# mLSTM denominators: the decayed scores are added over the key tiles on VectorE, and the ones matrix is multiplied with the one block of sums

## The chip, the cores and the metric

The kernel runs on one NeuronCore of a Trainium2 chip. The metric is device time in microseconds (us) of one execution, lower is better. TensorE (PE) multiplies matrices, VectorE (DVE) and ScalarE (ACT) do elementwise work, GpSimd (POOL) does some elementwise work and issues a few transfers, SyncE (SP) issues the weight loads. The engines run side by side and meet at semaphores.

## The reference

A trunk of two layers over 528 tokens (16 meta tokens and 512 of the sequence) with 1024 features. Layer 0 is an mLSTM mixer with 8 heads and a squared-ReLU MLP; layer 1 is differential attention and another MLP. What bears on the change is the denominator of the mLSTM:

```python
d_mat = jnp.exp(log_d - m_t[..., None])                        # decay, causal
s = jnp.einsum('bhctd,bhcsd->bhcts', qc, kc) * d_mat           # decayed scores
num = inter * (q @ C_prev) + einsum('bhcts,bhcse->bhcte', s, vc)
den = inter * (q @ n_prev) + jnp.sum(s, axis=-1)               # sum over the keys
hh = num / jnp.maximum(jnp.abs(den), jnp.exp(-m_t))[..., None]
```

The kernel computes it without chunks and carries: for each head a full causal table of decayed scores, 528 queries by 528 keys, whose sum over all keys is `den`.

## The kernel before

Everything is held transposed: features or keys on the 128 partitions, tokens along the row. Operands of TensorE that need full fp32 are split into a high and a low fp32r part, so that a product of a weight with an activation takes three passes (high·high, high·low, low·high). One weight unit is 128 output features: 8 blocks of 128 input features, 3 passes, 2 token halves of 264, thus 48 matmuls. `wh` and `wl` hold the two parts of a unit; ACT makes `wh` from the loaded `raw` (the copy in `split_unit`) and DVE subtracts to get `wl` (`split`, L814). The result of a unit is taken out of PSUM by DVE with `scaled` (L833). From head 1 on every unit of the mLSTM projections uses the same two PSUM banks 0 and 1, so that a unit can start only when the one before it has been taken out.

Each head has three units: unit 0 gives its q and k (to `qkf`), unit 1 its v (to `vf0`), unit 2 its output gate (to `of`). The eight heads are software-pipelined: the step of head hd does the scores and the outputs of head hd, and the three units of head hd+1. The order on each engine is written out by hand in the four functions `step0`. I call TensorE's stages in the step of head hd:

- **scores**: keys by queries (L1262), 14 matmuls, to `ps` banks 2 to 5
- **unit 0** of head hd+1: 48 matmuls
- **values**: the weighted sum of v, 21 matmuls (L1245 with `vh` and `vl`), after `p_ready`, to banks 6 and 7 (`B_ND`)
- **unit 1** of head hd+1, after DVE has taken unit 0 out
- **denominators**: the ones matrix times the decayed scores (L1245 with `ones_r`), 14 matmuls, to the same two banks as the values. It waits for `num_rd`: ACT has read the values.
- **unit 2, first half**: 24 matmuls, after DVE has taken unit 1 out (`evac`)
- **mean squares** over the features (L1294), 4 matmuls, after ACT has squared the denominators (`den_sq`) and DVE has made `sql`
- **unit 2, second half**, then the **transposes** of v (L1315), then the scores of head hd+1

The decayed scores of a head stand in `dmat`, 1360 columns: seven pieces, one for each key tile and query range of the causal table (`PIECES`, their first columns in `DCOL`). Five of them hold scores of queries from 256 on (of 272, 272, 272, 144 and 16 columns), the other two those of queries 0 to 255 and 128 to 255. DVE first fills `dmat` for the next head with exponents (`exponents`, 7 instructions, L899), ACT takes their exponential (L533), POOL masks the diagonal blocks (L437), and DVE multiplies by the scores (L912, L916). ACT then copies `dmat` to `phi` (three pieces) and DVE makes `plo` = `dmat` - `phi` (L923), after which `p_ready` is signalled.

In the step of a head DVE's order is: L912/L916, `plo`, take out unit 0 (`qkf`), finish the log-sigmoid of the gate (L931, waits for `lsig`), `exponents`, three subtractions for the stacked q and k (L942 to L944, wait for ACT's three copies), two `wl` splits, take out unit 1 (`vf0`), a third split, `sql`, and then the work on the denominators. ACT's order is: the three `phi` copies, three functions for the log-sigmoid (L555, L557, L559, the `lsig` chain), three copies of q and k, the exponential of `dmat`, two `wh` splits, the reading of the values (four instructions, L589 and L590, which signal `num_rd`), `sqh`, an exponential (L539), a third split, and the squares of the denominators (L602, L603).

Loops are register loops over pairs of heads (`heads_loop`): heads 1 to 6 run in the loop, heads -1, 0 and 7 outside. In the step of head 7 there is no next head, and the units are the first ones of the output projection.

Of the kernel before, what the change touches and what calls it, by code (L numbers as in the profile page):

```python
# [30 lines left out]
ALU = mybir.AluOpType  # L31
ACT = mybir.ActivationFunctionType
AX = mybir.AxisListType
F32 = mybir.dt.float32
# [71 lines left out]
def wait(eng, sem, value):  # L106

    if not isinstance(value, int) or value > 0:
        eng.wait_ge(sem, value)
# [20 lines left out]
def program(nc, a, out):  # L130
    with ExitStack() as ctx:
# [4 lines left out]
        def place(name, shape, dt, where, end):  # L136
            size = 2 if dt == BF16 else 4
            for n in shape[1:]:
                size *= n
            size = (size + 31) // 32 * 32  # L140
            assert where[0] + size <= end, (name, where[0] + size - end)
            t = nc.alloc_sbuf_tensor_at(name, shape, dt, offset=where[0])
            where[0] += size
            return t

        def new(name, shape, dt=F32):
# [43 lines left out]
        sqh, sql = (place(n, [P, T], F32R, w0, limit) for n in ("sqh", "sql"))  # L190
        dmat = place("dmat", [P, DW], F32, w0, limit)
        phi, plo = (place(n, [P, DW], F32R, w0, limit) for n in ("phi", "plo"))
        ks, qhs, qls, vh, vl, of, mbc, nmbc = (
            [place(f"{name}{par}", shape, dt, w0, limit) for par in range(2)]
            for name, shape, dt in (("ks", [P, T], F32R), ("qhs", [P, T], F32R), ("qls", [P, T], F32R),
# [37 lines left out]
        def sems(names):  # L233
            return [sem(n) for n in names.split()]
# [21 lines left out]
            "stack_hi stack_lo v_t dpre dexp dready emn_done")  # L256
        s_done, p_ready, pv_done, den_done, num_rd, den_sq, x_rd, ssq_done, t_rd = sems(
            "s_done p_ready pv_done den_done num_rd den_sq x_rd ssq_done t_rd")
        lsig, w_done, hln_done, e_done, rs_rd, z_mul, zh_rd, z_ready = sems(
            "lsig w_done hln_done e_done rs_rd z_mul zh_rd z_ready")  # L260

# [197 lines left out]
        def _(act):  # L459
# [81 lines left out]
            def step0(hd, par, pair):  # L541
                n1, nxt = hd + 1, exists(hd + 1)
                first = isinstance(hd, int) and hd < 0
                if exists(hd):

                    wait(act, den_done, hd)
                    for n, (c0, c1) in enumerate(P_CUTS):
                        act.wait_ge(p_done, hd * len(P_CUTS) + (n + 1))
                        rows = 16 if c0 == D_FULL else P
                        copy(phi[0:rows, c0:c1], dmat[0:rows, c0:c1]).then_inc(ph_done, 1)  # L550
                if exists(hd):

                    act.wait_ge(evac, hd * 3 + 3)
                    wait(act, w_done, hd)
                    nc.scalar.activation(tbuf[:, :], of[par][:, :], ACT.Abs).then_inc(lsig, 1)  # L555
                    act.wait_ge(lsig, hd * 3 + 1)
                    nc.scalar.activation(tbuf[:, :], tbuf[:, :], ACT.Exp, scale=-1.0).then_inc(lsig, 1)  # L557
                    act.wait_ge(lsig, hd * 3 + 2)
                    nc.scalar.activation(tbuf[:, :], tbuf[:, :], ACT.Ln, bias=1.0).then_inc(lsig, 1)  # L559
                if nxt:  # L560

                    act.wait_ge(evac, n1 * 3 + 1)
                    wait(act, s_done, hd)
                    copy(ks[1 - par][0:64, :], qkf[64:128, :])
                    copy(qhs[1 - par][0:64, :], qkf[0:64, :])
                    copy(qhs[1 - par][64:128, :], qkf[0:64, :]).then_inc(stack_hi, 1)
                    if first:

                        act.wait_ge(u_t, 1)
                        copy(ucol[:, 0:4, :], ps[:, B_SUM, 0:32].rearrange("p (s g) -> p s g", s=4))  # L570
                        copy(ucol[0:16, 4, :], ps[0:16, B_SUM, 32:40])
                        copy(gains[:, 32:56], ps[:, B_SUM, 64:88]).then_inc(ucol_rd, 1)
                    else:
                        decays(n1, par)
                        split_unit(n1 * 3 + 2, 2, 0, n1)
                    split_unit(n1 * 3 + 3, 0, 0, n1 + 1)
                elif exists(hd):

                    act.wait_ge(unit_done, U_OUT0)
                    split(U_OUT0 + 2, 2, 0)  # L580
                    split(U_OUT0 + 3, 3, 0)
                if exists(hd):

                    act.wait_ge(pv_done, hd + 1)

                    wait(act, z_ready, hd)
                    wait(act, ssq_done, hd)
                    for b, t0, t1 in ((B_ND, 0, QSPLIT), (B_ND + 1, QSPLIT, T)):
                        copy(nf[:, t0:t1], ps[:, b, 0:t1 - t0], gains[:, ds(hd + 32, 1)])  # L589
                        last = nc.scalar.activation(abuf[:, t0:t1], ps[:, b, 0:t1 - t0], ACT.Square)  # L590
                    last.then_inc(num_rd, 1)

                    act.wait_ge(num_rd, hd + 1)
                    copy(sqh[:, :], abuf[:, :]).then_inc(sq_hi, 1)
                if nxt:
                    if not first:
                        row(par, pair)
                        split_unit(n1 * 3 + 4, 1, 0, n1 + 1)
                if exists(hd):

                    act.wait_ge(den_done, hd + 1)
                    nc.scalar.activation(acc[:, 0:QSPLIT], ps[:, B_ND, 0:QSPLIT], ACT.Square)  # L602
                    nc.scalar.activation(acc[:, QSPLIT:T], ps[:, B_ND + 1, 0:T - QSPLIT], ACT.Square).then_inc(den_sq, 1)  # L603

                    act.wait_ge(t_rd, hd + 1)
                    nc.scalar.activation(acc[:, :], acc[:, :], ACT.Ln).then_inc(hln_done, 1)
                    act.wait_ge(e_done, hd + 1)
                    nc.scalar.activation(acc[:, :], acc[:, :], ACT.Exp).then_inc(rs_rd, 1)
                if nxt:

                    act.wait_ge(v_t, n1 + 1)
                    wait(act, pv_done, hd)
                    copy(vh[1 - par][:, 0:4, :], ps[:, B_ND, :].rearrange("p (s e) -> p s e", e=P))
                    copy(vh[1 - par][0:16, 4, :], ps[0:16, B_ND + 1, 0:P]).then_inc(vh_done, 1)
                if first:
                    split_unit(4, 1, 0, 1)
                    decays(0, 1)
                    row(1, -1)
                if exists(hd):
                    act.wait_ge(z_mul, hd + 1)  # L620
                    copy(ah[:, ds(hd, 1), :].rearrange("p o t -> p (o t)"), nf[:, :]).then_inc(zh_rd, 1)
# [184 lines left out]
        def _(dve):  # L806
# [86 lines left out]
            def exponents(n1, par, pair):  # L893
# [6 lines left out]
                                           ucol[0:rows, j, ds(n1, 1)], 0.0, ALU.subtract, ALU.max)  # L900
                last.then_inc(dpre, 1)

            def step0(hd, par, pair):
                n1, nxt = hd + 1, exists(hd + 1)
                first = isinstance(hd, int) and hd < 0
                if exists(hd):

                    dve.wait_ge(s_done, hd + 1)
                    dve.wait_ge(dready, hd + 1)
                    dm = dmat  # L910
                    for n, (b, w, c0) in enumerate(P_BANKS):
                        ins = V.scalar_tensor_tensor(dm[:, c0:c0 + w], ps[:, b, 0:w], SCORE_SCALE, dm[:, c0:c0 + w],  # L912
                                                     ALU.mult, ALU.mult)
                        if n in (1, 3):
                            ins.then_inc(p_done, 1)
                    V.scalar_tensor_tensor(dm[0:16, D_FULL:DW], ps[0:16, B_S0 + 3, 272:288], SCORE_SCALE,  # L916
                                           dm[0:16, D_FULL:DW], ALU.mult, ALU.mult).then_inc(p_done, 1)

                    wait(dve, den_done, hd)
                    for n, (c0, c1) in enumerate(P_CUTS):  # L920
                        rows = 16 if c0 == D_FULL else P
                        dve.wait_ge(ph_done, hd * len(P_CUTS) + (n + 1))
                        last = V.tensor_tensor(plo[0:rows, c0:c1], dm[0:rows, c0:c1],  # L923
                                               phi[0:rows, c0:c1].bitcast(F32), ALU.subtract)
                    last.then_inc(p_ready, 1)
                    if nxt:

                        scaled(n1 * 3, 0, ALL, qkf[:, :])

                    dve.wait_ge(lsig, hd * 3 + 3)  # L930
                    V.scalar_tensor_tensor(of[par][:, :], of[par][:, :], 0.0, tbuf[:, :], ALU.min, ALU.subtract).then_inc(w_done, 1)  # L931
# [250 lines left out]
        def _(pe):  # L1182
# [67 lines left out]
            def step0(hd, par, pair):  # L1250
# [28 lines left out]
                if exists(hd):  # L1279

                    pe.wait_ge(num_rd, hd + 1)
                    one = lambda rows, j: ones_r[0:rows, :]
                    weighted(par, ((one, False), (one, True)), den_done)
                if nxt:
                    part0(n1, 2, 0, 4)
                else:
# [322 lines left out]
```

## Time before, and the profile before

| what | value |
|---|---|
| median of 3 runs | 1306.67 us (1305.73 to 1308.74) |
| span of the profiled execution | 1303.2 us |
| median of the runs less that span | 3.5 us |
| TensorE busy | 1278.0 us, 98% of the span |
| VectorE busy | 682.4 us, 52% |
| ScalarE busy | 544.9 us, 42% |
| GpSimd busy | 65.8 us, 5% |
| mean granted TensorE clock | 0.995 |
| the eight mLSTM heads | about 46 to 246 us |

No time of its own is given for the profiled execution beside its span; the span goes from the first to the last instruction, and the runs' times lie 3.5 us above it. Busy shares are means over the whole kernel. In the timeline an instruction's row gives its start, its length and, in square brackets, how long the engine sat idle before it and what ended that. Matmuls and elementwise instructions overlap their successor's start, so the cost of one in a queue is the distance from its start to the next one's start, which is less than its length.

### The profile page before, as it was taken

The numbers are of one execution on the slowest core, as the hardware profiler recorded it, in microseconds if no ns is written. First come the engines' busy times: TensorE is split into PE (matmuls) and PEld (weight loads), VectorE is DVE, ScalarE is ACT, GpSimd is POOL, SyncE is SP. The second block draws the span as 40 slices with busy tenths as digits, with TensorE's granted clock in tenths as the row PEclk, the third lists the DMA queues.
The fourth block names the chain that finished last, engine by engine and source line by source line (L and its number), as shares of the span: only waits on it lengthen the run. The fifth ranks groups of instructions, "written<-read, shape, count | busy, mean of one in ns | idle before, by whom it ended". The sixth has DMA issues, their size and how long they took to land.

```text
span 1303.2 us, 20870 instructions
## 1 busy us (share of the span) xinstructions
PE 1278.0 (98%) x8381; PEld 1153.7 (89%) x8381; DVE 682.4 (52%) x992; ACT 544.9 (42%) x895; POOL 65.8 (5%) x90
## 2 busy tenths in 40 slices
PE   7999999999999999999999999998999999999997
PEld 6899999999999999999988888876888888888886
DVE  5877777654334334234556677663643343443443
ACT  4656655543214123123445566664532241231332
POOL 3321221000000000000000000000000000000000
PEclk9899999999999999999999999999999999999999
DMA  6352242222232322222321211210332323232311
GB/s 161 84 122 72 65 111 75 71 75 89 96 97 98 98 65 97 97 91 70 97 81 50 65 49 48 64 64 33 97 97 98 97 98 97 97 97 97 97 65 64
DMA packets 141574, 110.28 MB, mean 85 GB/s; under 512 B 22104, under 2 KB 139920, under 8 KB 141520
## 3 DMA queue, kind: packets, MB, share of 16 engines
q1 hardware_dynamic: 140000, 104.93, 26.2%
q0 software_dynamic: 1392, 4.49, 1.5%
q8 instruction: 39, 0.64, 0.2%
q14 instruction: 15, 0.12, 0.0%
q10 hardware_dynamic: 128, 0.09, 0.0%
HBM read 107.38 MB, written 2.13 MB: 84 GB/s over the span
## 4 chain that ended last, share of the span: by engine, by line
issue 53%; PE 42%; DVE 2%; ACT 1%; DMA 0%; POOL 0%; SPq 0%; DVEq 0%; POOLq 0%; ACTq 0%
PE ps L1196 38%; PE ps L1245 2%; PE ps L1262 1%; DMA raw<-in_mlstm_w_in_dram 0%; DVE wl L814 0%; POOL dmat L437 0%; DVE yl L856 0%; PE ps L1315 0%; PE ps L1348 0%; PE ps L1294 0%; ACT wh L461 0%; DVE fin L1178 0%; DVE h L841 0%; PE ps L1212 0%; POOL sql L454 0%
## 5 line engine op out<-in xcount | busy, mean ns | idle before, releaser
L1196 PE MATMUL ps<-yh,wh 128*128 128x264 f32 (+1 forms) x1472 | 368.1, 314 | 0.5 <-DVE wl L814 0.4
L1196 PE MATMUL ps<-yl,wh 128*128 128x264 f32 (+1 forms) x1472 | 361.7, 309 | 0.0
L1196 PE MATMUL ps<-yh,wl 128*128 128x264 f32 (+1 forms) x1472 | 360.8, 309 | 0.0
L461 ACT ACTIVATE wh<-raw 128x1024 fp32r<-128x1024 f32 x192 | 200.1, 1049 | 188.4 <-PE ps L1196 187.9
L814 DVE TENSOR_TENSOR wl<-raw,wh 128x1024 fp32r<-128x1024 f32 x192 | 240.1, 1254 | 55.3 <-ACT wh L461 53.3
L1196 PE MATMUL ps<-ah,wh 128*128 128x264 f32 (+1 forms) x960 | 257.6, 322 | 1.3 <-DVE al L1167 0.8
L1196 PE MATMUL ps<-al,wh 128*128 128x264 f32 (+1 forms) x960 | 257.0, 322 | 0.0
L1196 PE MATMUL ps<-ah,wl 128*128 128x264 f32 (+1 forms) x960 | 256.3, 321 | 0.0
L1196 PEld LDWEIGHTS ps<-yh,wh 128*128 128x128 f32 x1472 | 239.7, 189 | 17.2 <-issue 1.7
L1196 PEld LDWEIGHTS ps<-yh,wl 128*128 128x128 f32 x1472 | 239.2, 189 | 13.7
L1196 PEld LDWEIGHTS ps<-yl,wh 128*128 128x128 f32 x1472 | 239.5, 189 | 13.0 <-issue 0.2
L1196 PEld LDWEIGHTS ps<-ah,wh 128*128 128x128 f32 x960 | 159.7, 188 | 16.5 <-DVE al L1167 1.2
L1196 PEld LDWEIGHTS ps<-ah,wl 128*128 128x128 f32 x960 | 159.3, 188 | 13.7
L1196 PEld LDWEIGHTS ps<-al,wh 128*128 128x128 f32 x960 | 159.4, 188 | 13.3
L1003 DVE TENSOR_TENSOR h<-ps,h 128x528 f32<-128x528 f32 (+1 forms) x80 | 55.9, 699 | 213.8 <-PE ps L1196 213.8
L646 ACT ACTIVATE abuf<-tbuf 128x528 f32<-128x528 f32 (+1 forms) x64 | 40.9, 639 | 267.3 <-DVEq L1028 267.3
L1025 DVE SCALAR_TENSOR_TENSOR tbuf<-ps,rb 128x528 f32<-128x528 f32 (+1 forms) x64 | 44.8, 700 | 113.0 <-PE ps L1196 107.3
L1030 DVE TENSOR_TENSOR al<-abuf,ah 128x528 fp32r<-128x528 f32 (+1 forms) x64 | 44.9, 701 | 82.6 <-ACT ah L647 82.6
L461 ACT ACTIVATE yh<-h,gains 128x528 fp32r<-128x528 f32 (+1 forms) x32 | 23.4, 731 | 59.6 <-DVEq L1008 52.7
L697 ACT ACTIVATE e<-ps,stat 128x272 f32<-128x272 f32 (+3 forms) x48 | 26.6, 557 | 47.1 <-DVE stat L1084 44.9
L454 POOL TENSOR_TENSOR sql<-abuf,sqh 128x512 fp32r<-128x512 f32 x8 | 10.3, 1290 | 646.6 <-ACT sqh L461 646.6
L647 ACT ACTIVATE ah<-tbuf 128x528 fp32r<-128x528 f32 (+1 forms) x64 | 39.8, 622 | 0.0
(196 smaller groups left out, 1072.6 us busy)
## 6 DMA issues: line engine op xcount, KB each, us to landing
raw<-in_mlp_w_up_dram SPq DMA_DIRECT2D x32, 1024.0 KB, 5.2
raw<-in_mlp_w_down_dram SPq DMA_DIRECT2D x32, 1024.0 KB, 4.9
raw<-in_diff_w_in_dram SPq DMA_DIRECT2D x24, 512.0 KB, 3.8
raw<-in_mlstm_w_in_dram SPq DMA_DIRECT2D x16, 512.0 KB, 3.9
raw<-in_mlstm_w_in_dram SPq DMA_DIRECT2D x16, 256.0 KB, 4.1
raw<-in_mlstm_w_out_dram SPq DMA_DIRECT2D x3, 1024.0 KB, 4.9
raw<-in_diff_w_out_dram SPq DMA_DIRECT2D x3, 1024.0 KB, 5.0
mbc<-gate_rows POOLq DMA_DIRECT2D x8, 264.0 KB, 4.5
```

What stands on the lines that cost most here:

```text
L454: nc.gpsimd.tensor_tensor(sql1[:, :], abuf[:, NMETA:T], sqh1[:, :].bitcast(F32), ALU.subtract).then_inc(sq_lo1, 1)
L461: return nc.scalar.activation(o, i, ACT.Copy, scale=scale)
L646: nc.scalar.activation(abuf[:, t0:T], tbuf[:, t0:T], ACT.Square).then_inc(sqa_done, 1)
L647: nc.scalar.activation(ah[:, k, t0:T], tbuf[:, t0:T], ACT.Square).then_inc(ah_done, 1)
L697: nc.scalar.activation(dst, src, ACT.Exp, bias=stat[:, i % 2, c:c + 1], accum_out=stat[:, i % 2, 2 + c:3 + c]).then_inc(exp_done[c], 1)
L814: V.tensor_tensor(wl[:, k, :, :], raw[:, k // 2, :, P * (k % 2):P * (k % 2) + P], wh[:, k, :, :].bitcast(F32), ALU.subtract).then_inc(spli ...
L1003: ins = V.tensor_tensor(tokens(h[:, b, :], spans), src or banks(k, spans), tokens(h[:, b, :], spans), ALU.add)
L1025: V.scalar_tensor_tensor(tokens(tbuf[:, :], spans), banks(k, spans), 0.0, tokens(rb[:, :], spans), ALU.max, ALU.mult).then_inc(evac, 1)
L1030: V.tensor_tensor(al[:, k, t0:T], abuf[:, t0:T], ah[:, k, t0:T].bitcast(F32), ALU.subtract).then_inc(a_ready, 1)
L1196: last = mm(ps[:, bank + s, 0:w_], w[:, slot, kb, :], m[:, kb, t0:t0 + w_], start=(kb == 0 and n == 0), stop=(kb == CB - 1 and n == 2))
L1245: last = mm(ps[:, b, c:c + t1 - t0], what(rows, j), p, start=(b not in seen), stop=(n in (1, len(PIECES) - 1) and i == len(passes) - 1))
L1262: last = mm(ps[0:rows, b, c:c + t1 - t0], ks[par][:, s0:s0 + rows], q[:, t0:t1], start=(m == 0), stop=(m == 1))
```

## The change

The multiplication by the ones matrix sums over the 128 partitions, that is over the keys of one tile; PSUM accumulates over the tiles. After the change DVE first adds the pieces of `dmat` that belong to the same queries and different key tiles into one block `dsum` of 528 columns (`column_sums`: five additions and a copy, and three of the additions wait for the one before them). ACT copies `dsum` to the high part `dsh`, DVE subtracts to get the low part `dsl`, and TensorE multiplies the ones matrix by `dsh` and `dsl` in 4 matmuls where it had 14.

`column_sums` stands on DVE between `plo` and the taking out of unit 0; the subtraction for `dsl` stands right after unit 0. On ACT the copy to `dsh` stands between the `phi` copies and the log-sigmoid. TensorE waits for `dsl_done` beside `num_rd`. As `phi` and `plo` are now last read by the values, they wait for `pv_done` and no longer for `den_done`; `dsum` waits for `den_done`.

```diff
+        dsum_at = w0[0]
+        dsum = place("dsum", [P, T], F32, w0, limit)
+        dsl = place("dsl", [P, T], F32R, [dsum_at], limit)
+        dsh = place("dsh", [P, T], F32R, w0, limit)
...
 # ScalarE, step0
-                    wait(act, den_done, hd)
+                    wait(act, pv_done, hd)
                     for n, (c0, c1) in enumerate(P_CUTS):
                         act.wait_ge(p_done, hd * len(P_CUTS) + (n + 1))
                         rows = 16 if c0 == D_FULL else P
                         copy(phi[0:rows, c0:c1], dmat[0:rows, c0:c1]).then_inc(ph_done, 1)
+                if exists(hd):
+
+                    act.wait_ge(dsum_done, hd + 1)
+                    copy(dsh[:, :], dsum[:, :]).then_inc(dsh_done, 1)
                 if exists(hd):
 
                     act.wait_ge(evac, hd * 3 + 3)
...
 # VectorE
+            def column_sums(hd):
+                d = dsum
+                at = lambda n: dmat[:, DCOL[n]:DCOL[n + 1]]
+
+                wait(dve, den_done, hd)
+                V.tensor_tensor(d[:, 128:256], dmat[:, 128:256], at(1), ALU.add)
+                V.tensor_copy(d[:, 0:128], dmat[:, 0:128])
+                V.tensor_tensor(d[:, 256:528], at(2), at(4), ALU.add).then_inc(dsum_first, 1)
+                dve.wait_ge(dsum_first, hd * 3 + 1)
+                V.tensor_tensor(d[:, 256:528], d[:, 256:528], at(5), ALU.add).then_inc(dsum_first, 1)
+                dve.wait_ge(dsum_first, hd * 3 + 2)
+                V.tensor_tensor(d[:, 384:528], d[:, 384:528], at(3), ALU.add).then_inc(dsum_first, 1)
+                dve.wait_ge(dsum_first, hd * 3 + 3)
+                V.tensor_tensor(d[0:16, 512:528], d[0:16, 512:528], dmat[0:16, D_FULL:DW], ALU.add).then_inc(dsum_done, 1)
...
-                    wait(dve, den_done, hd)
+                    wait(dve, pv_done, hd)
                     for n, (c0, c1) in enumerate(P_CUTS):
...
                     last.then_inc(p_ready, 1)
+                    column_sums(hd)
                     if nxt:
 
                         scaled(n1 * 3, 0, ALL, qkf[:, :])
+
+                    dve.wait_ge(dsh_done, hd + 1)
+                    V.tensor_tensor(dsl[:, :], dsum[:, :], dsh[:, :].bitcast(F32), ALU.subtract).then_inc(dsl_done, 1)
 
                     dve.wait_ge(lsig, hd * 3 + 3)
...
 # TensorE, step0
                     pe.wait_ge(num_rd, hd + 1)
-                    one = lambda rows, j: ones_r[0:rows, :]
-                    weighted(par, ((one, False), (one, True)), den_done)
+                    pe.wait_ge(dsl_done, hd + 1)
+                    for b, t0, t1 in ((B_ND, 0, QSPLIT), (B_ND + 1, QSPLIT, T)):
+                        for m, d in enumerate((dsh, dsl)):
+                            last = mm(ps[:, b, 0:t1 - t0], ones_r[:, :], d[:, t0:t1], start=(m == 0), stop=(m == 1))
+                    last.then_inc(den_done, 1)
```

## Rows read from the trace of the kernel before

**Rows 1.** Timeline of TensorE, heads 2 and 3: start, length, line, operation, count.

```profile
116.73 0.51 PE L1196 MATMUL ps<-yh,wh 128*128 128x264 f32 x2
...
133.87 0.51 PE L1196 MATMUL ps<-yh,wh 128*128 128x264 f32 x2
...
139.83 0.28 PE L1245 MATMUL ps<-phi,ones_r 128*128 128x256 f32 x1
...
141.67 0.51 PE L1196 MATMUL ps<-yh,wh 128*128 128x264 f32 x2
...
144.70 0.28 PE L1294 MATMUL ps<-sqh,head_mean 128*128 128x256 f32 x1
...
145.20 0.41 PE L1196 MATMUL ps<-yh,wh 128*128 128x264 f32 x2
```

**Rows 2.** Timeline of VectorE, heads 3 and 4.

```profile
128.28 1.70 DVE L923 TENSOR_TENSOR plo<-dmat,phi 128x800 fp32r<-128x800 f32 x3 [0.18 <-ACT phi L461]
131.40 0.71 DVE L833 TENSOR_TENSOR qkf<-ps,rb 128x528 f32<-128x528 f32 x1 [1.43 <-PE ps L1196]
132.03 0.70 DVE L931 SCALAR_TENSOR_TENSOR of<-of,tbuf 128x528 f32<-128x528 f32 x1
132.64 1.69 DVE L899 TENSOR_SCALAR dmat<-mbc,ucol 128x256 f32<-128x256 f32 x7
...
136.78 2.95 DVE L814 TENSOR_TENSOR wl<-raw,wh 128x1024 fp32r<-128x1024 f32 x2 [0.28 <-ACT wh L461]
...
142.30 0.70 DVE L960 TENSOR_TENSOR sql<-abuf,sqh 128x528 fp32r<-128x528 f32 x1
...
153.34 1.70 DVE L923 TENSOR_TENSOR plo<-dmat,phi 128x800 fp32r<-128x800 f32 x3 [0.31 <-ACT phi L461]
```

**Rows 3.** Timeline of ScalarE, head 3.

```profile
134.37 1.33 ACT L533 ACTIVATE dmat<-dmat 128x1344 f32<-128x1344 f32 x1 [0.27 <-DVE dmat L899]
...
135.70 1.99 ACT L461 ACTIVATE wh<-raw 128x1024 fp32r<-128x1024 f32 x2
137.60 0.45 ACT L461 ACTIVATE nf<-ps,gains 128x256 f32<-128x256 f32 x1
...
138.59 0.37 ACT L590 ACTIVATE abuf<-ps 128x272 f32<-128x272 f32 x1
```

**Rows 4.** Timelines of ScalarE and VectorE, head 7: the log-sigmoid.

```profile
228.64 0.63 ACT L555 ACTIVATE tbuf<-of 128x528 f32<-128x528 f32 x1
...
230.65 0.71 DVE L931 SCALAR_TENSOR_TENSOR of<-of,tbuf 128x528 f32<-128x528 f32 x1 [0.77 <-ACT tbuf L559]
```

**Rows 5.** Groups by form, 60 to 260 us: count, busy us, mean ns.

```profile
L461 ACT ACTIVATE sqh<-abuf 128x528 fp32r<-128x528 f32 x8 | 5.2, 646 | 0.3
...
L912 DVE SCALAR_TENSOR_TENSOR dmat<-ps,dmat 128x272 f32<-128x272 f32 x14 | 5.4, 431 | 0.0
```

**Rows 6.** Timeline of VectorE: instructions that wait for their predecessor on VectorE.

```profile
40.10 0.70 DVE L885 TENSOR_TENSOR gnm<-gb,gm 8x528 f32<-8x528 f32 x1
40.83 0.42 DVE L887 TENSOR_SCALAR gnm<-gnm 8x528 f32<-8x528 f32 x1
...
254.64 1.23 DVE L814 TENSOR_TENSOR wl<-raw,wh 128x1024 fp32r<-128x1024 f32 x1 [0.15 <-DVE h L1003]
```

**Rows 7.** Timelines of VectorE and TensorE, head 0.

```profile
54.40 1.70 DVE L923 TENSOR_TENSOR plo<-dmat,phi 128x800 fp32r<-128x800 f32 x3 [0.18 <-ACT phi L461]
...
66.87 0.52 PE L1196 MATMUL ps<-yh,wh 128*128 128x264 f32 x2
```

**Rows 8.** Timelines of GpSimd in head 3 and of VectorE in head 7.

```profile
135.88 4.35 POOL L437 TENSOR_TENSOR dmat<-dmat,causal 128x128 f32<-128x128 f32 x5 [14.95 <-ACT dmat L534]
...
231.60 2.36 DVE L814 TENSOR_TENSOR wl<-raw,wh 128x1024 fp32r<-128x1024 f32 x2 [0.24 <-ACT wh L461]
```

**Rows 9.** Windows: busy us of PE, PEld, DVE, ACT, POOL; PEclk; DMA share; GB/s.

```profile
42.00:44.00 2.00, 0.77 (x9) 0.52 (x7) 1.21 (x3) 1.95 (x5) 1.03 (x3) 1.00 0.10 17
...
48.00:50.00 2.00, 2.00 (x12) 1.92 (x11) 2.00 (x7) 1.08 (x1) 0.00 (x0) 0.50 0.75 166
```

More of the change, by code:

```diff
@@ L258, in program @@
             "s_done p_ready pv_done den_done num_rd den_sq x_rd ssq_done t_rd")
+        dsum_first, dsum_done, dsh_done, dsl_done = sems("dsum_first dsum_done dsh_done dsl_done")
         lsig, w_done, hln_done, e_done, rs_rd, z_mul, zh_rd, z_ready = sems(
```

## The prediction

> **What bounds the kernel now.** I read the page first, for the busy shares, then the timeline of TensorE in the mLSTM heads, then those of VectorE and ScalarE beside it. TensorE is busy for 98% of the span (the table above). In the heads it goes without a gap: the first half of unit 2 starts at 116.73 in head 2 and at 141.67 in head 3, a period of 24.94 us, in which one stage begins where the last one ends [rows 1]. So time taken from TensorE there counts in full, as long as DVE and ACT keep up. How near they are to being late is the question, and it is read stage by stage in head 3.
>
> After `plo` ends (128.28 + 1.70 = 129.98) DVE idles 1.43 us until unit 0 is finished, at 131.40 [rows 2]. ACT reads the values until 138.59 + 0.37 = 138.96 [rows 3], and the denominators, which wait for that in the same banks, start at 139.83 [rows 1]: 0.87 us to spare. `sql` is done at 143.00 [rows 2] and the mean squares want it at 144.70 [rows 1]: 1.70 us to spare. These are the covers that an insertion in front of them eats.
>
> **What the change takes away.** The denominators take 139.83 to 141.67, 1.84 us for 14 matmuls. Four matmuls of the same two widths are there to compare: the mean squares, 144.70 to 145.20, 0.50 us [rows 1]. TensorE is spared 1.34 us a head, 10.7 us in eight.
>
> **What it adds on DVE.** Two-input fp32 work costs 0.70 us for 528 columns [rows 2] and 0.43 for 272 [rows 5]: 1.05 ns a column over a fixed part, so 0.28 for 128 columns, 0.30 for 144, 0.16 for 16. Without a wait the next one starts 0.09 us before the end (132.03 + 0.70 against 132.64) [rows 2]; behind a wait for its own predecessor it starts 0.03 after (40.10 + 0.70 against 40.83) [rows 6]. The column sums, with the copy priced as an addition: -0.09 + 0.19 + 0.19 + 0.43, then 0.03 + 0.43, 0.03 + 0.30, 0.03 + 0.16, together 1.70 us from the end of `plo`. `dsum` is ready at 131.68. Unit 0 is then taken out 0.2 us later than before, still over by 132.3, and unit 1 wants it at 133.87 [rows 1]: hidden. `dsl` is another 0.70, and lies in a gap that the next point opens.
>
> **What it moves on ACT.** This is where I expect the price. The log-sigmoid ran on ACT while DVE made `plo`. Now the copy to `dsh` stands ahead of it and waits for the sums, and everything behind it in ACT's queue and, through `lsig`, behind L931 in DVE's waits too. I take 0.04 us for the handover (exponents end 132.64 + 1.69, ACT starts 134.37 [rows 2, 3]), so ACT starts the copy at S = 131.72. From S on, in head 3:
>
> - the copy: 0.65 [rows 5] less the overlap of 0.09 = 0.56
> - from the first log-sigmoid function to L931, as in head 7, where DVE did wait for it: 230.65 - 228.64 = 2.01 [rows 4]
> - L931 to the exponents 0.61 [rows 2], exponents to ACT's exponential 1.73 [rows 2, 3], that one to the first `wh` copy 1.33 [rows 3]: now S + 6.24 = 137.96, where the trace has 135.70
> - copy to DVE's `wl` split 1.08, the two splits 2.95 - 0.09 = 2.86 [rows 2, 3], taking out unit 1 as long as unit 0, 0.71 [rows 2], and 0.06 to TensorE (my estimate, between the handovers of 0.03 and 0.15 [rows 6]): S + 10.95 = 142.67
>
> ACT's three copies of q and k fit between L931 and the exponential, and DVE's three subtractions before the split, as now. Unit 2 can start at 142.67 where it started at 141.67 [rows 1]. On the way the reading of the values starts 1.90 after the `wh` copies and takes 1.36 [rows 3]: over at 141.22, so the denominators start at 141.28 instead of 139.83, end at 141.78, and TensorE stands again until 142.67. Idle 1.45 + 0.89 against 1.34 spared: 1.00 us lost. The shortening is swallowed, because the stage behind it waits for DVE and not for the denominators.
>
> **What is late next.** `sql` comes as much later as the reading of the values, 2.26 us, and the mean squares 1.00 later; the difference, 1.26, is less than the 1.70 to spare. The weight loads have no wait or issue of their own changed; they wait for `wl` splits that come about 2 us later, with most of a head to go before their data is wanted. After unit 2's start the rest of the loop is as before: from there to the end of the next `plo` it was 13.25 us (116.73 to 129.98) and 13.37 (141.67 to 153.34 + 1.70) [rows 1, 2], mean 13.31. The new period is 13.31 + 1.70 + 0.04 + 10.95 = 26.00 us against 24.94: 1.06 us a head. The numerator's operands, `phi` and `plo`, are not behind the sums and stay in time.
>
> **The sum.** Heads 1 to 6: 6.4 us. Head 0 begins with DVE nearer to TensorE: its `plo` ends at 54.40 + 1.70 = 56.10, and 56.10 + 1.74 + 10.95 = 68.79 against 66.87 [rows 7]: 1.9 us. Head 7 has no next head and so no unit 1 to wait for; between 0 and the 1.0 of another head I take 0.3, since its own wait for the values stays. That is 8.6; I take 8.0, because the pair of splits went in at a long value. It is 2.36 us where GpSimd does nothing and 2.95 here, where it works on the masks from 135.88 to 140.23 [rows 2, 8]; after the change masks and splits move together. The profiled execution would go from 1303.2 to 1311.2 us of span, and with the 3.5 us that the median lies above that, 1314.7 us.
>
> The Trainium skill says of this (GPSIMD Engine Reference, section Specifications) that GpSimd shares its SBUF interfaces with VectorE and that the two contend when a DVE instruction has two SBUF inputs. The splits agree, 2.95 against 2.36. The sums have two SBUF inputs as well, but stand where GpSimd has no work; if its masks lay over them they would be a quarter longer, 0.4 us a head more.
>
> **Bounds.** Low: the splits at 2.36 (-0.59) and the three waits of the sums free (-0.36), so 0.11 a head, 1.0 in head 0, none in head 7: 1.6 us, 1308.3. High: each wait in the sums 0.15 (the widest handover on DVE itself [rows 6]) instead of 0.03, +0.36 a head, 2.5 over seven heads, and head 7 at 1.0: 8.0 + 2.5 + 0.7 = 11.2, 1317.9.
>
> **The rivals.** About 0.2%, 2.6 us, is what a measurement of this kernel can tell from no change.
>
> *The spared matmuls come through.* Then 1306.67 - 10.7 = 1295.9 us. It needs the way from the end of `plo` to unit 2 to be 24.94 - 1.34 - 13.31 = 10.3 us or less; any gain needs less than 11.6, one that counts less than 11.3, and I work out 12.7. For it: DVE idles 1.43 and ACT has gaps. Against: each link is a row, and DVE's idle time lies before the point at which the log-sigmoid, moved behind the sums, becomes its releaser. 9%.
>
> *It evens out.* The low bound: shorter splits and free waits, 1308.3 or a little under. For it: the two splits vary by as much as the loss at stake. Against: it needs both at once. 10%.
>
> *The clock falls.* Before head 0 TensorE was busy for 0.77 of 2 us, and some us later, with the engine full again, the granted clock was 0.50, that is 1.2 instead of 2.4 GHz [rows 9]. If 2.3 us of idle time in each head did the same, a stage of unit 0's length (48 matmuls, 133.87 to 139.83, 5.96 us [rows 1]) would run partly at half speed: with half of it so, 3 us a head, 24 more, 1339 us. Against: the new gaps are split by matmuls and surrounded by 23 us of full work. 4%. The Trainium skill (TensorE: Matmul & The Clock Gate, What's actually happening) also has two levels and an engine that falls to the lower one after idling; the row bears out the fall.
>
> **How the numbers follow.** The forecast, the chain through the log-sigmoid binds, has 77%, with 1308.3 to 1317.9 as its own range. All of it above 1309.3 and the clock case are slower: 81%. Same: 10%. Faster: 9%. The range 1308.5 to 1318 leaves out the gain, the clock case and the ends of the bounds.
>
> **What would show it.** In the profile after: L1245 with `ones_r` gone and 4 matmuls of `dsh` and `dsl` in about 0.50 us; a period of about 26.0 us; TensorE idle in two places of each head, some 1.4 us before the denominators, released by ACT, and 0.9 before unit 2, released by DVE; DVE idle about 1.1 us before L931, until ACT L559 ends; `dsum` ready about 1.7 us after `plo`; the clock at 1.00. I am wrong if the sums are much shorter, if the splits fall to 2.4 us, or if TensorE's gap is elsewhere.

## The result, and the profile after

| | before | after |
|---|---|---|
| median | 1306.56 us (4 runs, 1305.73 to 1308.74) | 1324.12 us (4 runs, 1323.74 to 1325.26) |
| ratio | | 1.0129, 95% interval 1.0115 to 1.0144 |
| span of the profiled execution | 1303.2 us | 1323.6 us |
| mean granted TensorE clock | 0.995 | 0.985 |
| period of a head, from mean squares to mean squares, mean of heads 1 to 6 | 24.94 us | 27.42 us |

The change makes the kernel 17.6 us slower, 1.3%. I had forecast 8.0 us slower, 1314.7 us, with a range that ended at 1318.

The timeline of TensorE in the changed kernel, head 3; the first two rows answer to the denominators and unit 2 in [rows 1], the last to the mean squares:

```profile
149.90 0.38 PE L1313 MATMUL ps<-dsh,ones_r 128*128 128x256 f32 x1 [1.32 <-ACT abuf L599]
...
151.06 0.48 PE L1224 MATMUL ps<-yh,wh 128*128 128x264 f32 x2 [0.41 <-DVE vf L842]
...
155.57 0.28 PE L1325 MATMUL ps<-sqh,head_mean 128*128 128x256 f32 x1
```

Both gaps that the prediction named are there, the first released by ACT's reading of the values, the second by DVE taking unit 1 out. In most heads one of them or both are longer than in this one: the same stage in head 2, with the first matmuls of unit 2,

```profile
122.41 0.38 PE L1313 MATMUL ps<-dsh,ones_r 128*128 128x256 f32 x1 [1.45 <-ACT abuf L599]
...
122.87 0.29 PE L1313 MATMUL ps<-dsl,ones_r 128*128 128x272 f32 x1
123.88 0.48 PE L1224 MATMUL ps<-yh,wh 128*128 128x264 f32 x2 [0.72 <-DVE vf L842]
...
126.26 0.64 PE L1224 MATMUL ps<-yh,wh 128*128 128x264 f32 x2
126.70 0.64 PE L1224 MATMUL ps<-yl,wh 128*128 128x264 f32 x2
...
127.91 0.40 PE L1224 MATMUL ps<-yl,wh 128*128 128x264 f32 x2
128.15 0.41 PE L1224 MATMUL ps<-yh,wl 128*128 128x264 f32 x2
128.40 0.28 PE L1325 MATMUL ps<-sqh,head_mean 128*128 128x256 f32 x1
```

What to see: the four matmuls take about half a microsecond and the gap behind them 0.72 us. And then the pairs of matmuls of unit 2 start 0.44 us apart (126.26, 126.70) until shortly before the end, where they are 0.24 apart again (127.91, 128.15). The first half of unit 2 takes 123.88 to 128.40, 4.52 us, against 141.67 to 144.70, 3.03 us, before [rows 1]. The windows over exactly that stage, heads 0, 2, 3 and 4, show why; the columns are those of [rows 9]:

```profile
68.92:73.44 4.52, 4.51 (x24) 4.52 (x25) 2.46 (x3) 1.20 (x3) 0.84 (x2) 0.62 1.17 265
...
123.88:128.40 4.52, 4.52 (x24) 4.52 (x25) 2.46 (x3) 1.19 (x3) 0.57 (x1) 0.62 1.10 258
151.06:155.57 4.51, 4.51 (x25) 4.51 (x25) 2.46 (x3) 1.50 (x4) 0.55 (x2) 0.62 1.05 239
178.67:183.19 4.52, 4.52 (x24) 4.52 (x25) 2.46 (x3) 1.18 (x3) 0.69 (x2) 0.62 1.14 259
```

The granted clock is 0.62 over the stage. In windows of 1 us it is 0.50, the lower level of 1.2 GHz, in two or three of them in a row in each of heads 0 to 6, between 0.52 and 0.98 in the ones at either edge, and 1.00 in all others from 56 us on. Added up, 12 us of full clock are missing. In the kernel before none is in the same windows. At the lower level the pairs of matmuls take 0.44 us where they take 0.24 to 0.25 otherwise, and so the stage is 1.5 us longer in a head.

VectorE and ScalarE in head 3 of the changed kernel, which answer to [rows 2] and [rows 3]:

```profile
136.90 1.70 DVE L947 TENSOR_TENSOR plo<-dmat,phi 128x800 fp32r<-128x800 f32 x3 [0.18 <-ACT phi L466]
...
140.15 0.16 DVE L925 TENSOR_TENSOR dsum<-dsum,dmat 16x16 f32<-16x16 f32 x1
140.26 0.71 DVE L842 TENSOR_TENSOR qkf<-ps,rb 128x528 f32<-128x528 f32 x1
141.02 0.71 DVE L956 TENSOR_TENSOR dsl<-dsum,dsh 128x528 fp32r<-128x528 f32 x1
142.91 0.71 DVE L959 SCALAR_TENSOR_TENSOR of<-of,tbuf 128x528 f32<-128x528 f32 x1 [1.18 <-ACT tbuf L568]
...
147.67 2.62 DVE L823 TENSOR_TENSOR wl<-raw,wh 128x1024 fp32r<-128x1024 f32 x2 [0.28 <-ACT wh L466]
150.22 0.69 DVE L842 TENSOR_TENSOR vf<-ps,rb 128x528 f32<-128x528 f32 x1
```

```profile
140.34 0.65 ACT L466 ACTIVATE dsh<-dsum 128x528 fp32r<-128x528 f32 x1 [2.83 <-DVE dsum L925]
...
145.26 1.33 ACT L538 ACTIVATE dmat<-dmat 128x1344 f32<-128x1344 f32 x1 [0.40 <-DVE dmat L908]
...
146.59 1.99 ACT L466 ACTIVATE wh<-raw 128x1024 fp32r<-128x1024 f32 x2
```

The two splits of `wl` in a row take 2.62 us in heads 3 and 6 and 2.93 to 2.95 in the five others. From the end of `plo` (138.60) to ACT's copy (140.34) it is 1.74 us. From there it is 2.57 to L959, 4.92 to the exponential, 6.25 to the `wh` copies and 9.56 to the denominators. DVE idles 1.18 us before L959 until the log-sigmoid on ACT is done.

### The profile page after: what moved, and what is told of

It is laid out like the page before. It is cut to its first block, busy times and chain, and to the rows that moved or that the text cites. A ratio compares the mean times of both kernels' runs of the same rounds, so it can differ in the third digit from the quotient of the medians.

```text
span 1323.6 us, 20785 instructions
## 1 busy us (share of the span) xinstructions
PE 1282.3 (97%) x8301; PEld 1155.8 (87%) x8301; DVE 700.5 (53%) x1048; ACT 548.9 (41%) x903; POOL 65.8 (5%) x90
## 4 chain that ended last, share of the span: by engine, by line
issue 54%; PE 34%; DVE 7%; ACT 3%; POOL 1%; DMA 0%; DVEq 0%; ACTq 0%; POOLq 0%
PE ps L1224 32%; DVE wl L823 1%; DVE dmat L908 1%; DVE plo L947 1%; ACT wh L466 1%; DVE dmat L936 1%; POOL dmat L442 0%; ACT phi L466 0%; ACT tbuf L566 0%; ACT tbuf L568 0%; DMA meta_in<-in_meta_tokens_dram 0%; ACT tbuf L564 0%; DVE of L842 0%; DVE vl L1018 0%; DVE yl L865 0%
## 5 line engine op out<-in xcount | busy, mean ns | idle before, releaser
L1224 PE MATMUL ps<-yh,wh 128*128 128x264 f32 (+1 forms) x1472 | 372.9, 317 | 4.9 <-DVE vf L842 4.4
L1224 PE MATMUL ps<-yl,wh 128*128 128x264 f32 (+1 forms) x1472 | 366.3, 313 | 0.0
L1224 PE MATMUL ps<-yh,wl 128*128 128x264 f32 (+1 forms) x1472 | 365.0, 312 | 0.0
L1224 PEld LDWEIGHTS ps<-yh,wh 128*128 128x128 f32 x1472 | 244.1, 192 | 22.8 <-DVE wl L823 5.3
L1224 PEld LDWEIGHTS ps<-yl,wh 128*128 128x128 f32 x1472 | 244.4, 193 | 13.1 <-issue 0.2
L1224 PEld LDWEIGHTS ps<-yh,wl 128*128 128x128 f32 x1472 | 243.5, 192 | 13.8
```

The lines of the kernel that those rows point to most:

```text
L1224: last = mm(ps[:, bank + s, 0:w_], w[:, slot, kb, :], m[:, kb, t0:t0 + w_], start=(kb == 0 and n == 0), stop=(kb == CB - 1 and n == 2))
```

## The experiments

Two theories stood against each other for the size of the loss. One: the two gaps cost about 1 us a head, and the rest is the clock, which falls because of them. The other: the clock, or what slows unit 2, has a cause beside the gaps, such as the weight loads that land in the same stretch (DMA share 1.05 to 1.17 above).

### The gaps filled

Matmuls whose result nobody reads are put into both gaps; `fill(11)` stands before the wait for `num_rd`, `fill(5)` behind the denominators.

```diff
+                def fill(n):
+
+                    for _ in range(n):
+                        mm(ps[:, B_S0, 0:HALF], ones_r[:, :], yh[:, 0, 0:HALF], start=True, stop=True)
+                if exists(hd) and nxt:
+                    fill(11)
...
                     last.then_inc(den_done, 1)
+                if exists(hd) and nxt:
+                    fill(5)
```

> The changed kernel with matmuls of no use put into its two gaps on TensorE: 11 of 264 columns before the denominators and 5 behind them, into a bank of the scores that is free there. Theory: the changed kernel's 17.6 us are two things, the two waits (about 1.0 us a head, some 8 us in all) and a granted clock of 0.50 over the first half of unit 2 that follows from them (24 matmuls in 4.52 us instead of 3.03, 1.5 us a head). With the gaps filled the waits stay and the clock does not fall: 24 matmuls in about 3.0 us, the clock 1.00 there, 1313 to 1315 us. Rival: the clock falls for a reason that lies beside the waits (weight loads land in the same stretch, DMA share over 1.0): the clock is 0.50 there as in the changed kernel and the time stays at 1323 to 1325 us.

Measured: 1313.75 us, ratio to before 1.0058 (1.0041 to 1.0075), as the theory had it. The timeline and the windows of TensorE:

```profile
117.60 1.48 PE L1310 MATMUL ps<-yh,ones_r 128*128 128x264 f32 x11
119.20 0.39 PE L1319 MATMUL ps<-dsh,ones_r 128*128 128x256 f32 x1
...
119.79 0.78 PE L1310 MATMUL ps<-yh,ones_r 128*128 128x264 f32 x5
```

```profile
120.34:123.38 3.04, 3.04 (x27) 1.00 1.19 277
146.06:149.06 3.00, 3.00 (x26) 1.00 1.18 279
```

The first half of unit 2 takes 3.0 us at a clock of 1.00, while the DMA share in it is as high as in the changed kernel, 1.18 and 1.19. So the transfers do not slow it and do not pull the clock down. TensorE does 16 useless matmuls a head and the kernel is 10.4 us faster than the changed one. That is the clock's part: 1324.12 - 1313.75 = 10.4 us, which fits 1.5 us in each of seven heads. The part of the waits is what is left over the kernel before, measured beside this run at 1306.30: 7.4 us. By the starts of the mean squares it is 2.15 us in head 0, 0.83 in each of heads 1 to 6 (a period of 25.77 us) and 0.30 in head 7.

Two more runs fill one gap each.

```diff
-                if exists(hd) and nxt:
-                    fill(5)
```

> The changed kernel with the 11 matmuls of no use in the gap before the denominators only; the gap of about 0.7 us before unit 2 stays. Theory: the clock falls when enough idle time comes together around the denominators, and 0.7 us is not enough (lsig_first had gaps of 0.4 to 0.7 us there and the clock stayed up from head 1 on): clock 1.00, 1313 to 1315 us as with both gaps filled. Rival: the gap straight before unit 2 is the one that counts: the clock falls in every head, 1321 us or more.

```diff
-                if exists(hd) and nxt:
-                    fill(11)
```

> The changed kernel with the 5 matmuls of no use behind the denominators only; the gap of 1.3 to 1.5 us before them stays. Theory: that gap alone is near what is enough, as in sums_old_matmuls, where it stood alone and the clock fell in four of seven heads: it falls in some heads and not in others, 1316 to 1321 us. Rival: it needs both gaps: clock 1.00 and 1313 to 1315 us.

Measured: 1313.65 us (1.0051, 1.0035 to 1.0068) with the first gap filled, 1314.34 us (1.0056, 1.0037 to 1.0074) with the second. With the first filled the clock is at 1.00 from 56 us on, although 0.40 to 0.73 us of idle time remain before unit 2. In head 0 of this run there even are two gaps, 1.02 us left of the first and 0.71 before unit 2, and the clock stays up. With the second filled it falls in head 0 alone, where the gap before the denominators was 2.36 us; with 1.17 to 1.45 us in heads 1 to 6 it does not. So the forecast for the second run was wrong: the clock fell in one head where I had some, and the time is the rival's. From head 1 on it needed both gaps in this kernel.

### The sums made, the old matmuls kept

The copies to `phi` and the subtractions for `plo` wait for `den_done` again, as in the kernel before.

```diff
-                    for b, t0, t1 in ((B_ND, 0, QSPLIT), (B_ND + 1, QSPLIT, T)):
-                        for m, d in enumerate((dsh, dsl)):
-                            last = mm(ps[:, b, 0:t1 - t0], ones_r[:, :], d[:, t0:t1], start=(m == 0), stop=(m == 1))
-                    last.then_inc(den_done, 1)
+                    one = lambda rows, j: ones_r[0:rows, :]
+                    weighted(par, ((one, False), (one, True)), den_done)
```

> The changed kernel with the column sums, dsh and dsl all made and waited for, but the denominators computed by the 14 matmuls of before. TensorE has one gap a head, before the denominators, and behind them no wait for unit 1, since the 14 matmuls cover it. Theory (waits plus clock, and the clock needs the two gaps with only 4 matmuls between): period about 24.9 + 1.45 = 26.4 us at full clock, 1317 to 1319 us, which is faster than the changed kernel although TensorE has 1.34 us more work a head. Rival A: one gap of 1.45 us is enough for the clock to fall: 1327 to 1331 us. Rival B: the changed kernel's loss is not on the way to the denominators: the time is that of the changed kernel plus the 10 us of matmuls, 1334 us.

Measured: 1324.99 us, 1.0149 (1.0124 to 1.0174). None of the three numbers. The timeline of TensorE, heads 2 and 3, and windows behind the gap of each:

```profile
121.89 0.39 PE L1273 MATMUL ps<-phi,ones_r 128*128 128x256 f32 x1 [1.46 <-ACT abuf L599]
...
149.87 0.39 PE L1273 MATMUL ps<-phi,ones_r 128*128 128x256 f32 x1 [1.33 <-ACT abuf L599]
```

```profile
122.00:124.00 2.00, 2.00 (x15) 0.96 0.71 172
124.00:126.00 2.00, 2.00 (x10) 0.50 1.18 268
126.00:128.00 2.00, 2.00 (x13) 0.69 1.10 236
150.00:152.00 2.00, 2.00 (x15) 1.00 0.71 182
152.00:154.00 2.00, 2.00 (x17) 1.00 1.11 259
```

There is one gap, as forecast, and no wait for unit 1. The clock fell in heads 0, 2, 4 and 6 and stayed up in 1, 3 and 5: my 1318 us for the wait alone and some 6.8 us of lost clock, counted in windows of 1 us, give 1324.8. The kernel is as slow as the changed one although TensorE is given all its old work back. With the clock's part taken from both, some 1318 stand against 1313.7 us: the spared matmuls are worth 4 to 5 us of the 10.7, and the changed kernel loses most of that again because its clock falls in seven heads and not in four. Here the clock fell behind the gaps of 1.46 us (and of 2.32 in head 0) and not behind those of 1.19 and 1.33 us. But it stayed up behind 1.50 us in head 7, and behind 1.44 and 1.45 us in the run with the second gap filled. Why, I can't say; the kernels differ in the matmuls that follow.

### The matmuls spared, nothing added

The kernel before, with 4 matmuls of the first 528 columns of `phi` and `plo`. The sums over the key tiles are left out.

```diff
-                    one = lambda rows, j: ones_r[0:rows, :]
-                    weighted(par, ((one, False), (one, True)), den_done)
+                    for b, t0, t1 in ((B_ND, 0, QSPLIT), (B_ND + 1, QSPLIT, T)):
+                        for m, d in enumerate((phi, plo)):
+                            last = mm(ps[:, b, 0:t1 - t0], ones_r[:, :], d[:, t0:t1], start=(m == 0), stop=(m == 1))
+                    last.then_inc(den_done, 1)
```

> The kernel before with 4 matmuls for the denominators, of the first 528 columns of phi and plo, so that the sums over the key tiles are left out: nothing is added on VectorE and ScalarE. Full value theory (rival): 1.34 us a head come through, 1306.6 - 10.7 = 1296 us. Theory: the 14 matmuls of before covered the taking out of unit 1 (0.20 + 0.71 + 0.06 us after unit 1's last matmul), of which 4 matmuls cover only 0.50, so that at least 0.47 us a head comes back as a wait: 0.87 us a head gained, 1299 to 1301 us, TensorE idle 0.4 to 0.5 us before unit 2, released by L833; the clock stays at 1.00.

Measured: 1297.89 us, 0.9939 (0.9922 to 0.9955), between the two, nearer to the theory. The gap is there:

```profile
136.80 0.29 PE L1284 MATMUL ps<-plo,ones_r 128*128 128x272 f32 x1
137.49 0.48 PE L1196 MATMUL ps<-yh,wh 128*128 128x264 f32 x2 [0.40 <-DVE vf L833]
```

The old 14 matmuls covered the time in which DVE takes unit 1 out of the banks that unit 2 needs. Four don't: a wait of 0.40 us stands in their place, although nothing was added on DVE and ACT, and the period is 24.10 us, 0.84 less than before and not 1.34.

### The log-sigmoid first

```diff
 # ScalarE: the copy to dsh moves behind the log-sigmoid
-                if exists(hd):
-
-                    act.wait_ge(dsum_done, hd + 1)
-                    copy(dsh[:, :], dsum[:, :]).then_inc(dsh_done, 1)
...
                     nc.scalar.activation(tbuf[:, :], tbuf[:, :], ACT.Ln, bias=1.0).then_inc(lsig, 1)
+                if exists(hd):
+
+                    act.wait_ge(dsum_done, hd + 1)
+                    copy(dsh[:, :], dsum[:, :]).then_inc(dsh_done, 1)
 # VectorE: the subtraction for dsl moves behind the one that waits for lsig
```

> The changed kernel with the copy to dsh behind the three log-sigmoid functions on ScalarE, and the subtraction for dsl behind L959 on VectorE. Theory: the log-sigmoid, held up behind the sums, makes the 2.26 us by which everything on ScalarE is late. With it back in its old place VectorE is late only by what the sums push out unit 0's taking out (0.2) and by dsl (0.62), 0.8 us: the denominators start without a wait or nearly, one gap of 0.7 to 0.9 us stands before unit 2, the clock stays at 1.00, and the time is 1302 to 1305 us, a little faster than the kernel before. Rival: the price is VectorE's added work itself (2.4 us a head) and not the order: the waits shrink by less than half, 1313 us or more.

Measured: 1303.09 us, 0.9972 (0.9963 to 0.9982). TensorE in one head:

```profile
141.25 0.38 PE L1313 MATMUL ps<-dsh,ones_r 128*128 128x256 f32 x1
...
142.40 0.48 PE L1224 MATMUL ps<-yh,wh 128*128 128x264 f32 x2 [0.40 <-DVE vf L842]
```

The wait before the denominators is gone from head 1 on. The one before unit 2 is 0.40 us in this head and 0.71 to 0.73 in the others. The clock falls only in head 0, where the gaps are 0.91 and 0.71 us, and 21 us have come back by moving two instructions, with the same work on every engine. The order was the cause of the first gap, and through it of the clock.

### The rest of the way

Three steps, each on top of the last. First, `dsl` behind the three subtractions of the stacked q and k.

```diff
-                    dve.wait_ge(dsh_done, hd + 1)
-                    V.tensor_tensor(dsl[:, :], dsum[:, :], dsh[:, :].bitcast(F32), ALU.subtract).then_inc(dsl_done, 1)
+                    dve.wait_ge(dsum_done, hd + 1)
...
                                     ALU.subtract).then_inc(stack_lo, 1)
+                    if not first:
+                        low_sums(hd)      # the two lines above
```

> As lsig_first, and the subtraction for dsl stands on VectorE behind the three subtractions of the stacked q and k, where lsig_first had ScalarE waiting for VectorE's exponents. Theory: ScalarE and the wl splits are then late by the 0.2 us alone, unit 1 is taken out as soon as it is finished or 0.2 us later, TensorE's gap before unit 2 shrinks from 0.4 to 0.7 us to 0.4 to 0.5 us, head 0's wait before the denominators goes and its clock stays at 1.00: 1299 to 1302 us. Rival: what is left in lsig_first is VectorE's load and not the place of the subtraction: 1303 us again.

Measured: 1301.65 us, 0.9967 (0.9957 to 0.9978). The time is in the range, the mechanism is not the forecast one. The gap before unit 2 did not shrink to 0.4 to 0.5 us; it was 0.59 us in head 1 and 0.75 to 0.88 in heads 2 to 6. Head 0's wait before the denominators is gone, but its clock did not stay up: TensorE waited 2.38 us for `plo`, and the clock was at 0.50 from 58 to 64 us. The gap in head 3:

```profile
141.06 0.28 PE L1319 MATMUL ps<-dsl,ones_r 128*128 128x256 f32 x1
142.35 0.48 PE L1230 MATMUL ps<-yh,wh 128*128 128x264 f32 x2 [0.76 <-DVE vf L842]
```

What the denominators no longer wait for, unit 2 still does: `dsl` pushes the two splits instead, and behind them the taking out of unit 1. Second, then, DVE takes unit 1 out between the two splits, and makes `sql` before the third.

```diff
                         split(n1 * 3 + 2, 2)
-                    split(n1 * 3 + 3, 0)
-                    if not first:
 
                         wait(dve, v_t, n1)
                         scaled(n1 * 3 + 1, 0, ALL, vf0[:, :])
-                        split(n1 * 3 + 4, 1)
+                    split(n1 * 3 + 3, 0)
...
+                    if nxt:
+                        split(n1 * 3 + 4, 1)
```

> As dsl_late, and VectorE takes unit 1 out before the second wl split, with sql before the third. Theory: unit 1 is finished only when the denominators' 4 matmuls start, so the gap before unit 2 keeps a floor of 0.20 + 0.71 + 0.06 - 0.50 = 0.47 us, which dsl_late has nearly reached; nothing or at most 1.5 us is gained over it: 1298 to 1301 us. Rival (queueing on VectorE still holds unit 2 up): the gap shrinks by more and 3 us or more are gained.

Measured: 1297.38 us, 0.9949 (0.9932 to 0.9966), 4.3 us better. The rival had it right: the queue on DVE was still holding unit 2 up. Now the gap is the floor, 0.41 us in each of heads 1 to 6, and the time is that of the run which adds nothing on DVE at all (1297.89). The column sums are hidden. Third, unit 2 goes to banks 4 and 5, to be free of that floor; the scores' pieces in bank 4 wait until DVE has taken it out, in every head, where before only head 0 had such a wait.

```diff
-                blocks(n1 * 3 + j, j, yh, yl, ALL, 2 * j if first else 0, 0 if first else n1 * 3 + j, kb0, kb1)
+                bank, free = 2 * j if first else 4 if j == 2 else 0, 0 if first else n1 * 3 + (1 if j == 2 else j)
+                blocks(n1 * 3 + j, j, yh, yl, ALL, bank, free, kb0, kb1)
...
+                        if (b, c) == (B_S0 + 2, 0):
+                            pe.wait_ge(evac, hd * 3 + 3)
...
-                    scaled(n1 * 3 + 2, 0, ALL, of[1 - par][:, :])
+                    scaled(n1 * 3 + 2, 0, ALL, of[1 - par][:, :], ps[:, 4:6, 0:HALF])
```

> As vf_early, and unit 2 goes to PSUM banks 4 and 5, which the scores leave free, so that it need not wait until unit 1 has been taken out. Theory: this removes the floor, TensorE has no gap at the denominators, and the spared 1.34 us a head come through in full: a period of 23.6 us, 1294 to 1297 us. Rival: VectorE, which now has over 22 us of work in a head of 23.6, becomes late elsewhere (mean squares or the numerator's operands): a gap of TensorE shows at L1325 or before the values, and the time is 1298 us or more.

> The kernel before with unit 2 in banks 4 and 5 alone: the control for the bank part of the run above. Theory: before, the 14 matmuls cover the taking out of unit 1 and TensorE never waits there, so the banks are worth nothing: 1305 to 1308 us. Rival: the banks are worth something by themselves, 1303 us or less, and the gain of the run above isn't the sums' alone.

> vf_early_banks45 once more with more rounds: the changed kernel with the log-sigmoid first on ScalarE, dsl behind the stacked q and k, unit 1 taken out before the second split, and unit 2 in banks 4 and 5. Theory: the same as in its first run, 1293 to 1296 us, ratio 0.990 to 0.993. Rival: part of it was the execution's luck in head 0: 1297 us or more.

Measured: 1294.83 us, 0.9921 (0.9904 to 0.9937), and measured again 1293.94 us, 0.9903 (0.9887 to 0.9920). The banks alone, on the kernel before: 1305.74 us, 1.0003 (0.9993 to 1.0013). So the banks are worth nothing as long as the 14 matmuls cover the taking out. With both there is no gap at the denominators in heads 1 to 6, and the mean squares start every 23.45 us where it was 24.94. Of these 1.49 us, 1.35 come from the denominators, 1.84 us before and 0.49 now, and 0.08 from the first half of unit 2, which takes 2.95 us where it took 3.03. In the better kernel VectorE is just in time at the mean squares, which start at 139.30:

```profile
139.57 0.70 DVE L998 TENSOR_TENSOR acc<-acc,nmbc 128x528 f32<-128x528 f32 x1
140.38 0.42 DVE L1002 SCALAR_TENSOR_TENSOR acc<-acc,ps 128x256 f32<-128x256 f32 x1
```

L1002 reads the mean squares without having had to wait for them; before, DVE idled about 1.8 us at this place.

## Why the prediction was wrong

**The chain of waits was right.** In head 3 the column sums, forecast at 1.70 us from the end of `plo`, took 1.71. From ACT's copy on: to L959 2.57 forecast and 2.57 measured, to the `wh` copies 6.24 and 6.25, to the denominators 9.56 and 9.56, to unit 2 10.95 and 10.72. The last is the only one that is off: the two splits took 2.62 us there, where I had 2.95. In five of the seven heads they took 2.93 to 2.95, and unit 2 came after 11.02 to 11.04 us. TensorE's gaps, forecast 1.45 and 0.89, were 1.16 to 1.45 and 0.40 to 0.72 in heads 1 to 6. DVE's idle time before L959, forecast about 1.1, was 1.18. With the gaps filled and the clock up, the kernel takes 7.4 us more than before, and the forecast was 8.0: head 0 has 2.15 against 1.9, heads 1 to 6 have 0.83 each against 1.06, head 7 has 0.30 against 0.3. In that run the splits were short in five of the seven heads. The cut from 8.6 to 8.0 us "because the pair of splits went in at a long value" fits that run. In the changed kernel itself the long value was the usual one, so that the last 0.6 us came out so well is luck.

**The step that failed is the clock.** The sum put its cost at nothing. It was the rival with 4%, put aside because "the new gaps are split by matmuls and surrounded by 23 us of full work". Neither kept the clock up. It fell in all seven heads that have a unit 2, and cost 10.4 us, by the filled gaps. The price of that rival was too high as well, 24 us: the clock was down for 3 to 4 us behind each pair of gaps, at half speed, so 1.5 us a head and not 3. The trace of the kernel before could have told. [rows 9] shows the fall before head 0 in windows of 2 us, where it looks like one long stretch of little work. By instruction it is this:

```profile
42.56 0.21 PE L1307 MATMUL ps<-ident,more_rows 24*128 24x24 f32 x1
44.25 0.77 PE L1315 MATMUL ps<-ident,vf 128*128 128x128 f32 x5 [1.48 <-ACT gains L461]
46.07 0.58 PE L1262 MATMUL ps<-qhs,ks 128*128 128x256 f32 x1 [1.06 <-DVE qls L944]
```

TensorE is full until 42.8 us, idles 1.48 us, does five transposes and idles 1.06 us, and the clock is 0.78 from 45 to 46 and 0.50 from there to 52. These are two gaps of the size that I forecast, 1.45 and 0.89 us, and split by matmuls too.

**The order as the cause** was argued in the prediction and is now shown: with the log-sigmoid first, the loss of 17.6 us is a gain of 3.2, at the same work.

**The full gain was never there.** The rival "the spared matmuls come through" was priced at 1.34 us a head, and needed only a short enough chain in its working. I had not seen that the 14 matmuls covered the emptying of banks 0 and 1. The run with nothing added shows a 0.40 us wait in their place; only the other banks brought out the rest.

**"It evens out"** needed shorter splits and free waits at once. The splits were shorter, 2.62, in two of seven heads only, and the waits on DVE were 0.03 to 0.04 us as the sum had them.

## What to carry to other kernels

When work is inserted into a queue whose engine has idle time, look at what stands behind it and was overlapped until then: here the added 2.4 us a head could be hidden in full, and in the first order they made the kernel 17.6 us slower. Removing matmuls can uncover a wait that they covered, so ask of each removed instruction what ran beside it. And where a change leaves TensorE with new gaps of a microsecond or more, price the clock too: filling them with matmuls that nobody reads is a quick test, and tells the clock's share from that of the wait.

## What the runs showed of the hardware

- Behind two gaps of 1.16 to 1.45 and 0.40 to 0.72 us, with four matmuls (0.5 us) between them, in an engine otherwise full for 24 us, the granted clock went to 0.50 in each of heads 1 to 6. Behind a single gap of 0.40 to 0.88 us it did not, in any of heads 1 to 6 of five kernels. Behind a single one of 1.17 to 1.46 us it did in one kernel in three of six heads and in another in none. And in head 0 it fell behind 0.91 and 0.71 us in one kernel and stayed up behind 1.02 and 0.71 us in another.
- It is not the same from one execution to the next where gaps lie near what is enough. At the start of head 0, with the same gaps of 1.5 and 1.1 us in front, the profiled executions of the kernel before and of the changed one had 0.50 from 46 us on, and the kernel before with unit 2 in banks 4 and 5 had 1.00 until 57 us. There TensorE came to the values early, waited 2.40 us for `plo`, and only then the clock fell. The windows of that run:

```profile
48.00:50.00 2.00, 2.00 (x19) 2.00 (x18) 2.00 (x6) 1.24 (x2) 0.00 (x0) 1.00 0.83 187
...
54.00:56.00 2.00, 0.00 (x0) 0.00 (x0) 1.83 (x6) 1.97 (x5) 0.00 (x0) 1.00 0.94 154
...
58.00:60.00 2.00, 2.00 (x9) 1.72 (x9) 1.96 (x7) 1.58 (x3) 0.00 (x0) 0.50 0.03 8
```

3.4 us of full clock are missing either way. At the start they cost little, because TensorE would wait for `plo` in any case: the values start at 56.43 us in the kernel before and at 56.01 in that run. Behind the wait they come on top: head 0's mean squares start at 69.89 and at 72.60 us. So the same fall can cost 2.7 us more by where it lands, which is part of the spread of this kernel's times, 1304.63 to 1309.55 us in ten runs.
